# Second MLP product of token groups 1 and 2 as seven block products in five passes, in a two-layer diffusion backbone on one Trainium2 core

## The reference, cut to what matters

```python
def sq_relu_mlp(h, w1, w2):
    return jnp.square(jax.nn.relu(h @ w1)) @ w2

    # in adaln_layer, with w1 (1024, 4096) and w2 (4096, 1024):
    h = rms_norm(x, norm_g[2]) * (1 + sc2) + sh2
    x = x + gt2 * rms_norm(sq_relu_mlp(h, w1, w2), norm_g[3])
```

## Time and profile before

| what | value |
|---|---|
| median of 3 runs | 2782.84 us |
| the profiled execution's own time | 2780.66 us |
| its span | 2778.9 us |
| PE busy | 2675.1 us, 96% |
| DVE busy | 1608.3 us, 58% |
| ACT busy | 1285.3 us, 46% |
| POOL busy | 312.8 us, 11% |
| mean granted TensorE clock | 0.993 |
| moved by DMA | 372.86 MB |

### The profile page before, as it was taken

The page is one execution under the profiler, slowest core; times in us unless marked ns, Lnnn a source line. Parts: engine busy times, 40 slices in busy tenths (PEclk is TensorE's granted clock), DMA queues, the critical chain, the costliest instruction groups (busy, mean ns, idle before and its releaser), DMA issues.

```text
span 2778.9 us, 37923 instructions
## 1 busy us (share of the span) xinstructions
PE 2675.1 (96%) x14835; PEld 2351.4 (85%) x14835; DVE 1608.3 (58%) x2516; ACT 1285.3 (46%) x2216; POOL 312.8 (11%) x308
## 2 busy tenths in 40 slices
PE   5999999999999999999999998889999999999998
PEld 3878888889998999878898886777899989998787
DVE  4246666564567775555522458985645577764444
ACT  5134445554444444444423676764544444443433
POOL 0000000000001222000000007971000002220000
PEclk8999999999999999999999999999999999999999
DMA  7743332633333444554413451025334434436554
GB/s 274 213 152 96 98 98 70 190 119 124 121 122 121 121 127 165 172 192 169 145 46 102 144 167 53 1 70 200 118 121 122 123 113 125 130 124 205 177 191 146
DMA packets 238909, 372.86 MB, mean 134 GB/s; under 512 B 24806, under 2 KB 181932, under 8 KB 237708
## 3 DMA queue, kind: packets, MB, share of 16 engines
q1 hardware_dynamic: 232496, 352.71, 40.0%
q10 hardware_dynamic: 4220, 9.86, 1.0%
q0 software_dynamic: 2016, 7.86, 0.7%
HBM read 329.88 MB, written 40.50 MB: 133 GB/s over the span
## 4 chain that ended last, share of the span: by engine, by line
PE 86%; DVE 5%; ACT 4%; DMA 2%; issue 2%; SPq 1%; POOL 0%; DVEq 0%; ACTq 0%; POOLq 0%
PE ps L2467 39%; PE ps L2580 16%; PE ps L2545 9%; PE ps L2281 8%; PE ps L2649 4%; PE ps L2242 3%; PE ps L2335 2%; PE ps L2362 1%; PE ps L2298 1%; DVE t_g L1790 1%; PE ps L2745 1%; ACT prT L1072 1%; SPq L622 1%; DVE xx L2105 1%; ACT junk_n L1139 1%
## 5 line engine op out<-in xcount | busy, mean ns | idle before, releaser
L1601 DVE TENSOR_TENSOR p_lo<-p_raw,p_hi 128x1024 fp32r<-128x1024 f32 x379 | 465.6, 1231 | 378.9 <-ACT p_hi L983 378.1
L983 ACT ACTIVATE p_hi<-p_raw 128x1024 fp32r<-128x1024 f32 x379 | 397.4, 1051 | 232.4 <-DMA p_raw<-mlp_w 121.7
L902 POOL TENSOR_TENSOR c_out<-c_out 128x384 f32<-128x384 f32 x128 | 117.9, 932 | 1601.7 <-ACT c_out L1257 1601.7
L2467 PE MATMUL ps<-p_hi,hq_hi 128*128 128x512 f32 x768 | 238.7, 392 | 4.8 <-DVE t_g L1790 4.8
L2467 PE MATMUL ps<-p_hi,hq_lo 128*128 128x512 f32 x768 | 236.7, 389 | 0.0
L2467 PE MATMUL ps<-p_lo,hq_hi 128*128 128x512 f32 x768 | 236.6, 389 | 0.0
L1262 ACT ACTIVATE hq_hi<-hq_raw 128x384 fp32r<-128x384 f32 x128 | 67.0, 523 | 268.9 <-DMA hq_raw<-hid_scratch 268.7
L2580 PE MATMUL ps<-t_hi,w_hi 128*128 128x384 f32 x512 | 173.2, 338 | 10.8 <-DVE t_g L1790 7.6
L1953 DVE TENSOR_TENSOR hq_lo<-hq_raw,hq_hi 128x384 fp32r<-128x384 f32 x128 | 71.9, 562 | 187.6 <-ACT hq_hi L1262 187.5
L2580 PE MATMUL ps<-t_lo,w_hi 128*128 128x384 f32 x512 | 172.9, 338 | 0.0
L2580 PE MATMUL ps<-t_hi,w_lo 128*128 128x384 f32 x512 | 172.9, 338 | 0.0
(11 more groups left out here) (298 smaller groups left out, 6050.0 us busy)
## 6 DMA issues: line engine op xcount, KB each, us to landing
p_raw<-mlp_w SPq DMA_DIRECT2D x256, 512.0 KB, 3.4
mod_p<-mod_w SPq DMA_DIRECT2D x80, 512.0 KB, 4.2
w_pair<-mlp_w SPq DMA_DIRECT2D x32, 1024.0 KB, 5.8
p_raw<-gla_w_in SPq DMA_DIRECT2D x56, 512.0 KB, 3.6
hid_scratch<-c_out SPq DMA_DIRECT2D x128, 192.0 KB, 1.9
hq_raw<-hid_scratch SPq DMA_DIRECT2D x128, 192.0 KB, 3.4
p_raw<-gla_w_out SPq DMA_DIRECT2D x24, 512.0 KB, 3.4
mod_w<-mod_w SPq DMA_DIRECT2D x8, 1024.0 KB, 19.0
```

What stands on the lines that cost most here:

```text
L902: nc.gpsimd.tensor_tensor(c_out[n % 4][:], c_out[n % 4][:], c_out[n % 4][:], ALU.mult).then_inc(c_squared, 1)
L983: nc.scalar.activation(p_hi[s][:, :, 0:width], p_raw[s][:, :, 0:width], ACT.Copy).then_inc(pan_hi, 1)
L1601: V.tensor_tensor(p_lo[s][:, :, 0:width], p_raw[s][:, :, 0:width], p_hi[s][:, :, 0:width].bitcast(F32), ALU.subtract).then_inc(pan_lo, 1)
L2467: mm = M.matmul(acc(slot)[:, cols], x, flat(w[s])[:, cols], start=begin and edge == 0, stop=end and edge == 2)
```

## The change

The second product of groups 1 and 2 becomes a two-by-two block product as well: hidden slices 2j and 2j+1 for one dimension, the output halves for the other, and the two groups for the third. It needs seven block products in place of eight, so 56 panels (HELD) take the place of 64. They run in five passes over the hidden width, kinds 0 to 4 with 16, 16, 8, 8 and 8 panels. The seven combinations of the hidden blocks are made in the pair jobs and stored; the combinations of the weights are made by DVE when a panel has landed. Five accumulated results are combined by DVE into group 1 (`xn`) and group 2 (`pp`).

In the pair jobs:
- ACT squares each block itself, right after its ReLU (a second instruction that waits for the first).
- POOL, in place of four squares, makes four sums or differences of blocks of 128 x 384 (`block_sums`), the first after three squares, the others after the fourth.
- SP stores seven blocks a job in place of four; ACT's ReLU of a job waits for POOL's sums of the job before.

In the held stage:
- SP brings 512 KB of weights a panel (256 KB in pass 1; in passes 2 to 4 two half rows of 2 KB) and 384 KB of hidden rows in place of 192 KB.
- DVE makes one difference of weights a panel in passes 0 to 3 (`sum_held`, 128 x 512 in passes 0 and 1, 128 x 1024 in 2 and 3), splits rows of 128 x 768 (`split_rows`) and the panel. ACT rounds 128 x 768 rows and the panel; in passes 0 and 1 in two halves, and the half that is a difference waits for DVE.
- At the end of pass 0 ACT copies the three accumulators into `pp`; after passes 1 to 4 DVE adds them (`pass_read`), with two more adds a tile in pass 2 (`shared_sums`). Group 1's `post_square` and `post_add` stand at panels 49 to 51.
- The operand of group 0 for the projection is turned at panels 6, 9, ... 27, that of group 1 no longer in the held stage but after parts 0 to 3 of the projection, that of group 2 after parts 4 to 7. The parts run four panels with group 0, then four with group 1.
- In the last job the first two held panels are prepared by ACT at steps 4 and 6, in place of 3 and 5; DVE stays at 3 and 5.

The diff, cut to its core:

```diff
+        PASSES = (0, JOBS, 2 * JOBS, 5 * JOBS // 2, 3 * JOBS)
+        HELD = 7 * JOBS // 2
+        HX0_STEPS = [6 + 3 * c for c in range(DC)]
...
+                def blocks_out(j):
+                    n = 4 * (JOBS * layer + j)
+                    s1, s2, s4 = s_out[layer]
+                    sp.wait_ge(c_squared, n + 2)
+                    sp.dma_start(hid_d[j, 6], c_out[1][:]).then_inc(hid_out[1], 16)
...
+                    sp.wait_ge(s_made, n + 4)
+                    sp.dma_start(hid_d[j, 3], s4[:]).then_inc(hid_out[3], 16)
...
-            def square_blocks(layer):
-                for n in range(4 * JOBS):
-                    pool.wait_ge(c_relu, 4 * JOBS * layer + n + 1)
-                    nc.gpsimd.tensor_tensor(c_out[n % 4][:], c_out[n % 4][:], c_out[n % 4][:], ALU.mult).then_inc(c_squared, 1)
+            def block_sums(layer, j):
+                n = JOBS * layer + j
+                q11, q22, q21, q12 = (x[:] for x in c_out)
+                s1, s2, s4 = (x[:] for x in s_out[layer])
+                pool.wait_ge(c_squared, 4 * n + 3)
+                if n:
+                    pool.wait_ge(hid_out[3], HID_BASE + 64 * n)
+                nc.gpsimd.tensor_tensor(s1, q11, q21, ALU.add).then_inc(s_made, 1)
+                pool.wait_ge(c_squared, 4 * n + 4)
+                pool.wait_ge(s_made, 4 * n + 1)
+                nc.gpsimd.tensor_tensor(q11, q12, q11, ALU.subtract).then_inc(s_made, 1)
+                nc.gpsimd.tensor_tensor(s2, s1, q12, ALU.subtract).then_inc(s_made, 1)
+                pool.wait_ge(s_made, 4 * n + 3)
+                nc.gpsimd.tensor_tensor(s4, q22, s2, ALU.subtract).then_inc(s_made, 1)
...
                 n = JOBS * layer + j
                 if n:
-                    act.wait_ge(hid_out[k], HID_BASE + 16 * n)
+                    act.wait_ge(s_made, 4 * n)
+                    act.wait_ge(hid_out[k], HID_BASE + (64 if k == 3 else 16) * n)
...
                 nc.scalar.activation(c_out[k][:], x, ACT.Relu).then_inc(c_relu, 1)
+                act.wait_ge(c_relu, 4 * n + k + 1)
+                nc.scalar.activation(c_out[k][:], c_out[k][:], ACT.Square).then_inc(c_squared, 1)
...
+            def sum_held(layer, n):
+                kind, j = pass_of(n)
+                if kind == 4:
+                    return
+                s, value = panel_landed[layer, n]
+                dve.wait_ge(pan_in[s], value)
...
+                V.tensor_tensor(out, x, y, ALU.subtract).then_inc(pan_summed, 1)
...
+            def pass_read(layer, kind, t):
+                dve.wait_ge(acc_done[t], acc_count(layer, t, kind + 1))
+                dve.wait_ge(acc_read[t], acc_count(layer, t, kind))
+                x = acc(t)
+                if kind == 1:
+                    last = V.tensor_tensor(xn[:, t, :], pp[layer][:, t, :], x, ALU.add)
+                elif kind == 2:
+                    last = V.tensor_tensor(xn[:, t, LEFT], xn[:, t, LEFT], x[:, RIGHT], ALU.add)
+                elif kind == 3:
+                    V.tensor_tensor(xn[:, t, LEFT], xn[:, t, LEFT], x[:, LEFT], ALU.add)
+                    last = V.tensor_tensor(xn[:, t, RIGHT], u_sum[:, t, :], x[:, LEFT], ALU.add)
+                else:
+                    last = V.tensor_tensor(pp[layer][:, t, LEFT], pp[layer][:, t, LEFT], x[:, RIGHT], ALU.add)
+                last.then_inc(acc_read[t], 1)
...
-                for n in range(HELD_ROWS):
+                for n in range(HELD):
+                    for kind in (1, 2):
+                        if n == PASSES[kind + 1]:
+                            for t in range(GT):
+                                pass_read(layer, kind, t)
+                    if n + 2 < HELD:
+                        sum_held(layer, n + 2)
+                        split_rows(layer, n + 2)
+                    if 0 < n - PASSES[2] <= GT:
+                        shared_sums(layer, n - PASSES[2] - 1)
+                    if 0 <= n - PASSES[4] < GT:
+                        pass_read(layer, 3, n - PASSES[4])
+                    if 0 < n - PASSES[4] <= GT:
+                        post_add(layer, 1, 1, n - PASSES[4] - 1)
...
+                    if n + 2 < HELD:
                         split_held(layer, n + 2)
```

More of the change, by code:

```diff
@@ L729, in mlp_panels @@
                         pair_in(j + 2)
-                    for k in range(4):
-                        block_out(j, k)
+                    blocks_out(j)
                 last_job = start + PRODUCTS * (JOBS - 1)
@@ L1136, in post_square @@
                 slot = OUT_SLOTS[g][t] if part == 0 else t
-                act.wait_ge(acc_done[slot], T.next(acc_done[slot]))
+                x = acc(slot)
+                if part and g:
+                    act.wait_ge(acc_read[t], acc_count(layer, t, (None, 4, 5)[g]))
+                    x = (None, xn, pp[layer])[g][:, t, :]
+                else:
+                    act.wait_ge(acc_done[slot], T.next(acc_done[slot]))
                 i = 3 * g + t
-                own(nc.scalar.activation(junk_n[:], acc(slot), ACT.Square, scale=1.0 / 32, accum_out=st_n[:, layer, 2 * part, 0, i:i + 1]))
+                own(nc.scalar.activation(junk_n[:], x, ACT.Square, scale=1.0 / 32, accum_out=st_n[:, layer, 2 * part, 0, i:i + 1]))
                 nc.scalar.activation(st_n[:, layer, 2 * part, 1, i:i + 1], st_n[:, layer, 2 * part, 0, i:i + 1], ACT.Sqrt,
@@ L1788, in post_add @@
                 gate = (gate1, gate2)[part][layer][:, 0 if i == 0 else 1, :]
+                if part and g:
+                    own(V.scalar_tensor_tensor(out=t_g[:], in0=(None, xn, pp[layer])[g][:, t, :], scalar=r, in1=gate, op0=ALU.mult,
+                                               op1=ALU.mult))
+                    x = xt[layer][:, i, :]
+                    V.tensor_tensor(x, x, t_g[:], ALU.add).then_inc(x_new, 1)
+                    return
                 slot = OUT_SLOTS[g][t] if part == 0 else t
@@ L1957, in pairs, with shared_sums @@
+            def shared_sums(layer, t):
+                second = pp[layer][:, t, RIGHT]
+                dve.wait_ge(acc_read[t], acc_count(layer, t, 2))
+                own(V.tensor_tensor(u_sum[:, t, :], xn[:, t, LEFT], second, ALU.add))
+                own(V.tensor_tensor(second, xn[:, t, LEFT], xn[:, t, RIGHT], ALU.add))
             def pairs(layer):
@@ L1983, in pairs @@
                         elif step in (3, 5):
+                            sum_held(layer, step // 2 - 1)
+                            split_rows(layer, step // 2 - 1)
                             split_held(layer, step // 2 - 1)
@@ L2219, in _ @@
             for t in range(GT):
+                pass_read(1, 4, t)
+            for t in range(GT):
                 i = 6 + t
```

295 lines of the change are left out of this document (203 added, 92 removed).

## The result

The changed kernel takes 2828.57 us (median of 4 runs, 2824.26 to 2830.93), the kernel before 2781.52 in the same comparison (4 runs, 2779.90 to 2783.64): 1.0167 times as long, 95% interval 1.0149 to 1.0185. It is slower by 47 us, where 11 was forecast; 2828.57 lies above the range of 2765 to 2811. The sign and the mechanism named as decisive were right, the size was not. The profiled execution took 2824.26 us, its span is 2822.5, so 43.6 us more than the 2778.9 of before.

What follows compares the result with a forecast made beforehand. PE, busy 96% of the span, was taken as the bound. Removed -71.5, held stage +21.9, projection +5.6, tail +1.8 gave -42 us; pair jobs +53 made it +11: 2794 us, range 2765 to 2811.

Steps and rivals of the forecast that it cites:

- Removed: Held stage: eight panels a layer, 65.3 us, and PE's stop between groups 1 and 2, 6.2 us; sum -71.5 us.
- the 3.1: Between groups 1 and 2: PE's stop waiting for DVE's post_add, 3.1 us a layer, would go.
- Pair jobs, the step that decides: Pair jobs: POOL's sums collide with DVE's, `c_sum`(0) ends at 11.99 where 10.18 was due; +53 us in both layers.
- PE waits 1.8 us in each job: Pair jobs: PE stops before product 4 for `c_sum`(0), 1.8 us a job; job 1 counts 3.2.
- The steady state: Held stage: DVE, ACT and DMA work for a panel stays hidden under PE's 4.08 us, with 4 us to spare.
- Layer 0, panel 4: 2.5 us: Held stage, layer 0: three pre_squares on ACT and three pre_scales on DVE come before both have caught up; 2.5 us.
- The start: Start of the held stage, both layers: late rows of panel 0 and late last `c_sum`; 3.7 us each.
- the ends of passes: Held stage: late pass_reads or ACT's late copy stop PE before passes 1 to 3; 4.5 us layer 0, 2.6 layer 1.
- the last pass: Held stage, panels 49 to 51: DVE's rows, adds and post_add exceed 4.08 us; 2.6 us late layer 0, 2.3 layer 1.
- Projection: Projection after layer 0: PE waits 3.4 us for group 1's last chunk and 2.2 for group 2's; +5.6 us.
- third rival, slow held rows: Held stage: landings 1.5 us later than taken, stops grow, +26 us in all, 2809 us; chance 0.10.
- Tail: End of the kernel: three pass_reads stand ahead of DVE's chain, the last starting when PE ends; +1.8 us.

Runs made afterwards that it cites:

- the dose of columns: Changed kernel with GpSimd's four sums on 192 or 2 of 384 columns: 2779.18 and 2757.11 us; with ScalarE's squares on 2 columns: 2799.75 us.
- The kernel with `c_sum`(0) first: Changed kernel with VectorE's first block sum of a job moved ahead of the third sum of weights and the next job's piece 0 split; 2767.25 us.
- the one with 2 columns of sums: Changed kernel, order kept, with GpSimd's four sums made on 2 columns of 384; 2757.11 us.
- the kernel of 2727.41 us: The kernel with `c_sum`(0) first plus reordered loads, stores, splits, reads, post_adds and transposes across the stages; 2727.41 us, ratio 0.9806 to the kernel before.
- the kernel of 2726.63: The kernel of 2727.41 us with layer 1's last group summed into PSUM, ScalarE copying the right half, scaling reading PSUM; 2726.63 us, one run.
- the kernel with the sums on VectorE: Changed kernel, order kept, with GpSimd's four block sums made by VectorE behind `c_sum`(0) of the next job; 2755.17 us.

## Why the prediction missed

**Removed.** 2016 matmuls with `hq` as forecast (3 x 672). The panels' 65.3 us went. Between the groups PE is idle for 2.4 us a layer (the gap between length and busy time); the 3.1 is the lateness of the third tile, and its other 0.7 is busy time, the modelled ends ahead of three stops and the slow first matmuls behind them. So the time was about right, but 1.4 us of it stand in the other column.

**Pair jobs, the step that decides.** Right in kind: POOL's sum is 1.01 us (1.00), `c_sum`(0) ends 11.90 us behind product 5 (11.99), PE idles 28 times. That all four of POOL's operations would collide was an estimate: rows 7 to 9 show three pairs that do. The trace of after shows all four (VectorE's four of the line take 1.08, 1.32, 1.50 and 1.49 us in place of 0.68, POOL's 1.01, 1.54, 1.46 and 1.33), and the dose of columns agrees. No run shows the port that the prediction and the expectations count with, and that both engines would read through. What the traces show is times: these operations, all inputs in SBUF, end 0.54 to 0.56 us (VectorE) or 0.86 to 0.87 us (GpSimd) behind the end of the other engine's operation that ran beside them, and `c_sum`, with one input in PSUM, keeps its time (0.56 us at 1025.38 in the kernel before, beside a square of 0.83 at 1025.18). What failed is the step from `c_sum`'s end to PE's time, "PE waits 1.8 us in each job" and 3.2 in job 1. That 1.8 is lateness against the due time, which already takes off the overlap of two matmuls, so what answers it is not the idle 1.76 but the 2.03 that the period grew by. That the table's 53.0 meets my 53.2 is luck: the one is idle time, the other lateness. Two things weren't in the sum, or not in full. The 0.15 us from the end of `c_sum`(0) to PE's start (0.06 was allowed for it, which no row shows) and the first matmul behind the stop, 0.25 us in place of 0.17, at granted clock 1.00, make up the 0.2 us by which an ordinary job is worse. And in job 1 PE is idle 3.4 us longer, but then runs at the lower level: 24 matmuls from start to start take 6.17 us (6.62 in layer 1) where they took 4.27 behind the stop of before. In the table's columns this is the 11.4 us: 0.27 for each of 26 ordinary stops (0.17 of the modelled end, 0.1 of the start) and 4.3 in the two jobs 1.

**Held rows.** The steady state held: hidden, between the ends of passes. The mis-sized step is "Layer 0, panel 4: 2.5 us": I saw the pre_scales and not that SP's loads stand behind the seventh store, nor that POOL's store starts at the same moment, though I had written down SP's seven stores, and POOL's sums, and costed them by their issue alone. It was 6.5 us in layer 0 and 2.7 in layer 1, where I had none. The start was 4.1 and 3.5 us, 2.3 of each for the last `c_sum` (3.7 forecast); the ends of passes 5.3 and 2.5 (4.5, 2.6), the last pass 1.9 and 1.7 (2.6, 2.3). All stops 28.4 against 21.9. The rest is busy time again: 59.3 us less where 65.3 of panels and 2.6 of 24 transposes (which moved to the projection) had gone, so 8.6 us more than the count of matmuls gives.

**Projection.** The stops are 5.8 us for 5.6, the first 3.44 for 3.4. Busy time is 5.9 more, of which the 24 transposes are 2.6 and 3.3 mostly the lower level: the 24 behind the first stop took 5.69 us in place of 4.17.

**Tail.** 3.4 us for 1.8. I had DVE's scalings at the old price, and forgot that their input now came from SBUF, where they collide as the operations of the pair jobs do: the second takes 3.46 us beside GpSimd's add of 2.33, 1.28 in the kernel before.

**The sum of the miss**: 23.3 us of busy time that no term held (11.4 + 8.6 + 3.3), 6.5 + 1.4 in the held rows, 1.6 in the tail, together 32.8; the spans say 32.6. Of the 23.3, by the starts of PE's matmuls, some 13 are what the lower level cost; some 10 are the modelled ends ahead of stops and the first matmuls behind them. A further 2.1 us is that the profiled execution lies 4.3 below the median in after and 2.2 in before. My third rival, slow held rows, had the right stage but not the mechanism: the median landing rose by 0.4 us for panels (3.4 to 3.8) and 0.9 for rows, not by 1.5.

**Open.** The kernel with `c_sum`(0) first has as few long stops as the one with 2 columns of sums, yet 12 us more busy time (2632.1 against 2620.0), partly between the layers, far from the change (granted clock 0.97 from 1600 to 1800 there and 0.96 to 0.98 in the kernels built on it, 1.00 in after and before, with the same instructions). That part of PE's clock isn't explained. The post_add moved in the pair jobs might help the kernel before by its 1.5 us too; that wasn't tried.

## To carry to other kernels

When a kernel turns out slower because an engine with idle time is late, look first at what stands ahead of the late instruction in its queue and needn't: here one instruction's place in the queue was worth 61 us, more than the 47 that the change lost. Price every stop twice, its idle time and what it costs beside that, the uncovered end of the matmul ahead and what the matmuls behind take beyond their pitch (here 0.27 us for one of 1.76 us, 2.2 for one of 4.9). And before work goes to GpSimd, compare the time for which it blocks VectorE with what VectorE needs to do it: 0.87 against 0.55 us here.

## What the runs showed of the hardware

- Matmuls behind a stop of PE. In after, behind 1.76 us the granted clock stays at 1.00 in all ordinary jobs (905 to 1130 and 2340 to 2560 us), and only the first matmul is slow, 0.25 us for 0.17. Behind 3.44, 4.94 and 6.53 us PE runs at a granted clock of 0.50 at once, for 2.7, 4.0 and 4.9 us (a matmul of 384 columns each 0.32 us in place of 0.173, one of 512 columns 0.43 in place of 0.227). Behind a stop of 2.13 us in the kernel with `c_sum`(0) first it starts at 0.173 us a matmul and falls to a granted clock of 0.50 1 us later, for 3.3 us. The length of a stop doesn't tell which of these comes: in layer 1 of after one of 2.33 us (at 2572.91) is followed by 0.50 at once, for 2.7 us, one of 2.68 us (at 2591.01) by 1.00 throughout. What decides it, these runs don't show.
- A scalar_tensor_tensor of 1024 columns with its inputs in SBUF took 3.46 us beside GpSimd's add of 2.33, in after and in the kernel of 2727.41 us, and 1.28 from PSUM beside the same add in the kernel of 2726.63. By the timeline it had started 0.05 us ahead of the add, and ended 1.1 us behind it all the same. A tensor_tensor of 1024 columns with both inputs in SBUF took 2.15 us beside that add in the kernel before, 1.23 with GpSimd idle.
- Collisions link up: in after GpSimd and VectorE alternate, and from GpSimd's second sum on each operation of one (1.33 to 1.54 us) is stretched by the last of the other (1.32 to 1.50). VectorE's line from its first sum of weights to the end of `c_sum`(0) takes 5.40 us in after (1035.25 to 1040.65), and 3.15 with GpSimd idle, in the kernel with the sums on VectorE (1028.15 to 1031.30).
